# First mixer of a hybrid decoder step reordered: token mixing on GpSimd during the sort, second group of key scores behind the eighth head

## What is computed

```python
def ab_mixer(h, e, dsa_fn, shift_prev, S0, P):
    z = h @ P['ab_w_in'][e]
    q, k, v, qi, ki, wi, zb = split_cols(z, [...])
    ya = dsa_fn(e, q, k, v, qi, ki, wi)      # top-k keys by index scores, then softmax(q k) v over them
    yb, shift_new, S_new = rwkv7(zb, shift_prev, S0, e, P)
    y = jnp.concatenate([ya, yb], axis=-1) @ P['ab_w_out'][e]

def rwkv7(zb, shift_prev, S0, e, P):
    prev = jnp.concatenate([shift_prev[:, None], zb[:, :-1]], axis=1)
    z = zb + (prev - zb) * P['rwkv_mu'][e]                 # the token mixing
    r, k, v, xw, xa, xg = split_cols(z, [512] * 3 + [64, 64, 128])
    w_log = -softplus(-(w0 + tanh(xw) @ w2)) - 0.5         # decays
    a = sigmoid(a0 + xa @ a2)                              # rates
    g = sigmoid(xg) @ g2
    kk = k * P['rwkv_kk'][e]; kk = kk * rsqrt(max(sum(kk * kk), 1e-24))
    k = k * (1.0 + (a - 1.0) * P['rwkv_ka'][e])
    # scan over tokens with r, exp(-exp(w_log)), k, v, -kk, kk * a
```

## Time and profile before

| | |
|---|---|
| median of 3 runs | 1491.55 us (1486.3 to 1495.07) |
| the profiled execution | 1492.41 us |
| its span in the trace | 1490.6 us |
| PE busy | 95% of the span |
| DVE busy | 74% |
| ACT, POOL busy | 22%, 22% |
| granted TensorE clock, mean | 0.965 |

### The profile page before, as it was taken

The page is one execution under the profiler, slowest core; times in us unless marked ns, Lnnn a source line. Parts: engine busy times, 40 slices in busy tenths (PEclk is TensorE's granted clock), DMA queues, the critical chain, the costliest instruction groups (busy, mean ns, idle before and its releaser), DMA issues.

```text
span 1490.6 us, 28278 instructions
## 1 busy us (share of the span) xinstructions
PE 1420.3 (95%) x11458; PEld 1296.7 (87%) x11458; DVE 1096.9 (74%) x1410; ACT 327.1 (22%) x651; POOL 332.6 (22%) x277
## 2 busy tenths in 40 slices
PE   6999999999778998899999999999999999999997
PEld 6999999995333697899999999999997569999997
DVE  7977677667866746788777688768579577887764
ACT  3111102003323442221110221111202362211110
POOL 2533112001100011253321153322200002443210
PEclk9999999999977998999999999999999879999998
DMA  8443542665974102544427344426152315444142
GB/s 313 144 166 113 200 147 102 218 198 175 351 270 167 41 30 90 213 149 168 169 80 255 118 172 166 169 101 235 45 207 111 128 52 209 152 162 161 63 158 89
DMA packets 62699, 233.15 MB, mean 156 GB/s; under 512 B 9003, under 2 KB 18544, under 8 KB 45580
## 3 DMA queue, kind: packets, MB, share of 16 engines
q1 hardware_dynamic: 50426, 224.56, 41.9%
q10 hardware_dynamic: 11554, 6.37, 1.4%
q0 software_dynamic: 624, 0.87, 0.2%
HBM read 225.54 MB, written 6.10 MB: 155 GB/s over the span
## 4 chain that ended last, share of the span: by engine, by line
PE 49%; DVE 5%; POOL 2%; ACT 1%; DMA 1%; issue 1%; POOLq 0%; DVEq 0%; SPq 0%
PE psum L191 15%; PE psum L193 15%; PE psum L192 14%; DVE x L393 1%; DVE ring_r L186 1%; DVE pair_hi L177 1%; DMA ring<-in_w_gu 1%; DVE hidden_hi L389 1%; DVE rstd L297 1%; POOL hidden L305 0%; POOL hidden L307 0%; PE psum L351 0%; PE psum L2681 0%; DMA ring<-in_w_cd 0%; PE psum L235 0%
## 5 line engine op out<-in xcount | busy, mean ns | idle before, releaser
L191 PE MATMUL psum<-x_hi_r,pair_hi 128*128 128x288 f32 x1736 | 517.2, 298 | 5.5 <-DVE up L598 2.7
L193 PE MATMUL psum<-x_hi_r,ring_r 128*128 128x288 f32 x1736 | 515.8, 297 | 0.0
L192 PE MATMUL psum<-x_lo_r,pair_hi 128*128 128x288 f32 x1608 | 475.5, 296 | 0.0
L186 DVE TENSOR_TENSOR ring_r<-ring,pair_hi 128x2048 fp32r<-128x2048 f32 (+1 forms) x127 | 341.0, 2685 | 4.3
L191 PEld LDWEIGHTS psum<-x_hi_r,pair_hi 128*128 128x128 f32 x1736 | 329.6, 190 | 8.2 <-issue 7.7
L193 PEld LDWEIGHTS psum<-x_hi_r,ring_r 128*128 128x128 f32 x1736 | 329.2, 190 | 0.0
L192 PEld LDWEIGHTS psum<-x_lo_r,pair_hi 128*128 128x128 f32 x1608 | 304.0, 189 | 0.3
L191 PE MATMUL psum<-hidden_hi_r,down_hi 128*128 128x288 f32 x704 | 208.5, 296 | 0.0
L192 PE MATMUL psum<-hidden_r,down_hi 128*128 128x288 f32 x704 | 208.0, 295 | 0.0
L193 PE MATMUL psum<-hidden_hi_r,down_r 128*128 128x288 f32 x704 | 207.3, 294 | 0.0
L177 DVE CAST pair_hi<-ring 128x2048 fp32r<-128x2048 f32 (+1 forms) x126 | 161.2, 1279 | 11.0 <-DMA ring<-in_w_gu 9.8
(11 more groups left out here) (545 smaller groups left out, 1847.1 us busy)
## 6 DMA issues: line engine op xcount, KB each, us to landing
ring<-in_w_gu SPq DMA_DIRECT2D x88, 1024.0 KB, 4.8
down<-in_w_down SPq DMA_DIRECT2D x64, 704.0 KB, 4.3
ring<-in_w_ab SPq DMA_DIRECT2D x18, 1024.0 KB, 5.1
ring<-in_w_cd SPq DMA_DIRECT2D x12, 1024.0 KB, 6.0
ring<-in_cache_k SPq DMA_DIRECT2D x32, 256.0 KB, 4.6
index_keys<-in_cache_k SPq DMA_DIRECT2D x32, 256.0 KB, 7.8
index_keys<-in_cache_i ACTq DMA_DIRECT2D x64, 64.0 KB, 2.8
eight_pages_ds<-in_cache_v SPq DMA_DIRECT2D x16, 256.0 KB, 5.2
```

The source lines that it names most:

```text
L186: return eng.tensor_tensor(lo, a, hi.bitcast(F32), ALU.subtract)
L191: pe.matmul(out, w_hi, x_hi, start=start, stop=False)
L192: pe.matmul(out, w_hi, x_lo, start=False, stop=False)
L193: return pe.matmul(out, w_lo, x_hi, start=False, stop=stop)
```

## The change

Token mixing moves from DVE to POOL: 27 tensor operations in place on slabs 16 to 29, two slabs at a time, each waiting for the one before, behind POOL's loads and beside the sort. DVE keeps only the copy of the last tokens, and ACT's tanh, PE's decay products and DVE's `inputs` wait for all 27. On PE the third value projection goes behind the sample index scores, which now wait for two value copies; the second group of key scores goes from head 6 to head 7. On DVE six rounds of the sort run ahead of head 0 and the query copies behind these; `ROUNDS` changes; the first half of `select` (now `threshold`, to L2023) goes ahead of head 7; the sampled softmax takes both groups together. In branch B the decays' products come before the weights' transposes and the rates' products between them; the key norms' square root comes behind the three Exp; AR and BK are made in another order; sequences 4 to 7 are multiplied together, four at a time and not two, with key norms in the middle. SP sends key pages 2 and 3 first and page 1 and value 0 behind the third value projection, which also ends later for POOL's memset and loads.

```diff
+    def mixing(pool):
+        pool.wait_ge(S["mix_loaded"], 16 * 9)
+        pool.wait_ge(S["shift_ready"], 1)
+        zz = z[:, 16:30]
+        n = 0
+        def step(out_, in0, in1, op):
+            nonlocal n
+            if n:
+                pool.wait_ge(S["mixed"], n)
+            pool.tensor_tensor(out_, in0, in1, op).then_inc(S["mixed"], 1)
+            n += 1
+        def rates(j0, j1, w):
+            return mu[:, j0:j1].rearrange("p (j a) -> p j a", a=1).to_broadcast([P, j1 - j0, w])
+        d = shared[:, 0:2 * (TP - 1)].rearrange("p (j t) -> p j t", j=2)
+        for j in range(0, 14, 2):
+            pair = zz[:, j:j + 2]
+            step(d, pair[:, :, 0:TP - 1], pair[:, :, 1:TP], ALU.subtract)
+            step(d, d, rates(j, j + 2, TP - 1), ALU.mult)
+            step(pair[:, :, 1:TP], pair[:, :, 1:TP], d, ALU.add)
+        first = shared[:, 0:14].rearrange("p (j a) -> p j a", a=1)
+        step(first, zz[:, :, 0:1], rates(0, 14, 1), ALU.mult)
+        step(zz[:, :, 0:1], zz[:, :, 0:1], first, ALU.subtract)
+        ds = shared[:, 0:14 * NS].rearrange("p (j n) -> p j n", j=14)
+        d4 = shared[:, 0:14 * NS].rearrange("p (j b t) -> p j b t", j=14, t=TS)
+        zs = zz[:, :, TP:NT].rearrange("p a (b t) -> p a b t", t=TS)
+        step(d4[:, :, :, 1:TS], zs[:, :, :, 0:TS - 1], zs[:, :, :, 1:TS], ALU.subtract)
+        step(d4[:, :, :, 0], shiftT[:, :, :], zs[:, :, :, 0], ALU.subtract)
+        step(ds, ds, rates(0, 14, NS), ALU.mult)
+        step(zz[:, :, TP:NT], zz[:, :, TP:NT], ds, ALU.add)
+        assert n == MIXED
...
+        sp.wait_ge(A["ms_done"], 1)
+        sp.dma_start(g2, c.ins["g2"]).then_inc(S["par_loaded"], 16)
...
-    def inputs(dve, ln):
...
-        dve.tensor_tensor(D[:, :, 1:TP], zz[:, :, 0:TP - 1], zz[:, :, 1:TP], ALU.subtract).then_inc(S["shift_ready"], 1)
...
-        for j in [12, 13, 4, 5, 6, 7, 0, 1, 2, 3, 8, 9, 10, 11]:
-            ins = dve.scalar_tensor_tensor(zz[:, j], D[:, j], mu[:, j:j + 1], zz[:, j], ALU.mult, ALU.add).then_inc(S["mixed"], 1)
-        dve.wait_ge(S["mixed"], 14)
+        dve.tensor_copy(zlast[:, :, 1:1 + NB], zz[:, :, TP + TS - 1:NT:TS]).then_inc(S["shift_ready"], 1)
+    def inputs(dve, ln):
...
+        dve.wait_ge(S["mixed"], MIXED)
+        dve.wait_ge(c.stored, 48)
+        ln(dve.tensor_scalar(omka, ka, -1.0, 1.0, ALU.mult, ALU.add))
...
+        dve.tensor_tensor(e3, e2, e1, ALU.subtract).then_inc(S["kk_max"], 1)
+        dve.wait_ge(S["lora_out"], 2 * HP)
+        for h in range(HP):
+            last = dve.tensor_scalar(f3[:, h], av[:, h], ka[:, h:h + 1], omka[:, h:h + 1], ALU.mult, ALU.add)
+        ln(last)
+        ln(dve.tensor_tensor(k, k, f3[:, :, :], ALU.mult))
...
+        def scaled(slot_of, a):
+            for q in range(2):
+                for c0, c1, n in ((0, 4, L), (4, 5, NS)):
+                    cols = slice(c0 * L, c0 * L + (c1 - c0) * n)
+                    last = dve.tensor_tensor(BK[half(q), :, c0:c1, slot_of(q), 0:n],
+                                             a[half(q), :, cols].rearrange("p h (c l) -> p h c l", l=n),
+                                             e2[half(q), :, cols].rearrange("p h (c l) -> p h c l", l=n), ALU.mult)
+            return last
+        dve.wait_ge(S["w_done"], 3)
+        dve.wait_ge(S["zeroed"], 2)
+        dve.tensor_tensor(AR[:, 1, :, 0:NT], r, e1, ALU.mult)
+        scaled(lambda q: 1 - q, k)
...
+        dve.scalar_tensor_tensor(AR[:, 0, :, 0:NT], f1[:, :, :], -1.0, e3, ALU.mult, ALU.mult).then_inc(S["ar_done"], 1)
+        ln(dve.tensor_tensor(f2[:, :, :], f1[:, :, :], av[:, :, :], ALU.mult))
+        scaled(lambda q: q, f2).then_inc(S["bk_done"], 1)
...
+    def decay_inputs(act):
+        act.wait_ge(S["mixed"], MIXED)
+        act.activation(decay_in, decay_in, ACT.Tanh).then_inc(S["lora_in"], 1)
     def lora_out(act):
...
+            act.wait_ge(S["lora_sum"], HP + h + 1)
+            act.activation(av[:, h], early[h][:, 0:NT], ACT.Sigmoid, bias=a0[:, h:h + 1]).then_inc(S["lora_out"], 1)
...
+        act.wait_ge(S["kk_max"], 2)
+        act.activation(rows8, rows8, ACT.Sqrt).then_inc(S["root_done"], 1)
...
     def decay_products(pe):
         pe.wait_ge(S["mix_loaded"], 16 * 9)
-        pe.wait_ge(A["st_out"], 6)
-        pe.wait_ge(S["lora_in"], 2)
+        pe.wait_ge(S["lora_in"], 1)
+        pe.wait_ge(A["mb_done"], 6)
...
-ROUNDS = (0, 3, 14, 17, 28, 31, 33, 33, 33)
+ROUNDS = (6, 10, 14, 23, 27, 31, 33, 33, 33)
...
+            for u in range(4):
+                sp.wait_ge(S["is_sum"], 3 * u + 2)
+                load("cache_k", 2 + u // 2, KEY_SLOTS[2 + u // 2], range(4 * (u % 2), 4 * (u % 2) + 4))
+            sp.wait_ge(S["is_used"], 12)
             sp.wait_ge(c.pair_done, first + npairs + 2)
             load("cache_k", 1, KEY_SLOTS[1])
+            load("cache_v", 0, VALUE_SLOTS[0])
+            idx.read_numbers(sp, c, 6)
+            idx.read_numbers(sp, c, 7)
             sp.wait_ge(v_done, 3)
             c.store(sp, c.outs["v_p"], vtok[:, 0:2])
...
             rk.lora_loads(pool)
+            rk.mixing(pool)
             rk.zeros(pool)
...
-            values_in(2, range(KT))
...
-            pe.wait_ge(v_done, 3)
+            pe.wait_ge(v_done, 2)
...
             weigh(11)
-            pe.wait_ge(S["wi_done"], 1)
+            values_in(2, range(KT))
...
-                if h in (2, 6):
+                if h in (2, 7):
                     key_scores(h // 4)
...
+            rk.decay_products(pe)
             pe.wait_ge(S["pt_out"], 8)
...
             weights_transposed(0)
             pe.wait_ge(S["st_out"], 3)
+            pe.wait_ge(v_done, 3)
             pages_landed(range(4))
             sample_values(range(4), range(4)).then_inc(S["kv_used"], 1)
+            rk.rate_products(pe)
             weights_transposed(1)
             sample_values(range(4), range(4, NPG + 1)).then_inc(S["kv_used"], 2)
-            rk.decay_products(pe)
+            rk.key_squares(pe)
             pe.wait_ge(S["st_out"], 6)
+            rk.rates_taken(pe)
             pages_landed((4, 5))
-            sample_values((4, 5), range(3))
-            rk.key_squares(pe)
-            sample_values((4, 5), range(3, 6))
-            rk.rate_products(pe)
-            sample_values((4, 5), range(6, NPG + 1)).then_inc(S["kv_used"], 1)
-            pages_landed((6, 7))
-            sample_values((6, 7), range(2))
+            pe.wait_ge(kv_landed[4], 256)
+            sample_values(range(4, 8), range(4))
             rk.key_norms(pe)
-            sample_values((6, 7), range(2, NPG + 1)).then_inc(S["kv_used"], 1)
+            pe.wait_ge(kv_landed[5], 256)
+            sample_values(range(4, 8), range(4, NPG + 1)).then_inc(S["kv_used"], 2)
             rk.value_products(pe)
             heads_transposed(0)
...
             keys_out(1)
+            rk.decay_inputs(act)
...
             weights_out(0)
+            rk.lora_out(act)
             weights_out(1)
-            rk.lora_inputs(act)
-            rk.lora_out(act)
             rk.decays(act)
...
+            def sample_queries():
+                dve.wait_ge(S["qz_zero"], 2)
+                rk.last_tokens(dve)
...
+            def select():
...
+            for i in range(ROUNDS[0]):
+                top_eight(i)
+            sample_queries()
             for h in range(8):
+                if h == 7:
+                    threshold()
                 head(h)
...
             masked(0)
+            masked(1)
             largest(0)
-            masked(1)
+            largest(1)
             divided(0)
-            largest(1)
             divided(1)
```

More of the change, by code:

```diff
@@ L755 @@
 EXP_HALF = float(np.exp(-0.5))
+MIXED = 27
 Recurrence = namedtuple("Recurrence", (
-    "first_loads", "lora_loads", "zeros", "restricted_keys", "sample_decays", "rows_load", "last_loads", "stores", "inputs", "chunks", "lora_inputs", "lora_out", "decays", "chunks_out",
+    "first_loads", "lora_loads", "zeros", "restricted_keys", "sample_decays", "mixing", "last_tokens", "rates_taken", "rows_load", "last_loads", "stores", "inputs", "chunks", "decay_inputs", "lora_out", "decays", "chunks_out",
     "decay_products", "key_squares", "rate_products", "key_norms", "value_products", "chunk_products"))
@@ L1161, in decay_products @@
         pe.wait_ge(S["mix_loaded"], 16 * 9)
-        pe.wait_ge(A["st_out"], 6)
-        pe.wait_ge(S["lora_in"], 2)
+        pe.wait_ge(S["lora_in"], 1)
+        pe.wait_ge(A["mb_done"], 6)
+        pe.wait_ge(A["op_out"], 4)
         for h in range(HP):
-            pe.matmul(free[h][:, 0:NT], wa2[0:64, h * P:h * P + P], lw[0:64, 0], start=True, stop=True).then_inc(S["lora_sum"], 1)
+            pe.matmul(early[h][:, 0:NT], wa2[0:64, h * P:h * P + P], decay_in, start=True, stop=True).then_inc(S["lora_sum"], 1)
     def key_squares(pe):
@@ L1177, in rate_products @@
             pe.wait_ge(S["lora_out"], h + 1)
-            pe.matmul(free[h][:, 0:NT], wa2[64:128, h * P:h * P + P], z[64:128, Z_WA], start=True, stop=True).then_inc(S["lora_sum"], 1)
```

(11 more changed lines are left out.)

86 lines of the change are left out of this document (26 added, 60 removed).

## The result

| | before | changed |
|---|---|---|
| median of 20 runs | 1495.25 us (1486.3 to 1499.01) | 1488.01 us (1478.72 to 1493.12) |
| ratio of the times | | 0.995, 95% interval 0.9933 to 0.9967 |
| profiled execution, its span | 1492.41, 1490.6 us | 1493.08, 1491.3 us |
| first index scores | 364.75 | 359.63 |
| sort begins / merge | 378.82 / 421.40 to 427.05 | 373.90 / 417.47 to 426.44 |

The change gains 7.2 us in the medians, 5 to 10 by the interval, half a per cent. The forecast was 1482 us, a gain of 9.55 on the median at hand. Of the 6 us between 1482 and 1488, 3.7 are the start: the median of the kernel before is 1495.25 over 20 runs and was 1491.55 over the three at hand. The other 2.3 are gain that did not come. 1488 also lies outside the 1479 to 1485 that the forecast case gave as its own, though well inside the whole range of 1473 to 1494.

A forecast was written before the change was run, and what follows sets the result against it. PE, busy 95%, bounds the kernel outside the mixers; inside, the chunk products' start decides. 1.6 us at the first sampled values plus 8.2 behind them give 9.8: profiled 1492.4 becomes 1482.6, forecast 1482 us, range 1473 to 1494.

The forecast's parts named there:

- the forecast case: The main case for the whole kernel: 1482 us, own range 1479 to 1485, chance 0.42.
- Index scores and sort: Mixer's start: index scores at 359.2, 5.5 us earlier; sort about 5.4 earlier; merge starts at 416.
- Mixing on GpSimd: Token mixing on POOL: starts at 395, takes 30 us (bounds 27.6 and 32), ends at 425.
- The disturbance: GpSimd's mixing beside VectorE's merge: each waits for the other's instruction; merge 12 us (5.6 to 14.6), sort untouched.
- The rival of a sort that waits for GpSimd: Sort and mixing run by turns, merge ends 15 us later; 1497 or 1510 us, middle 1502, chance 0.12.
- a merge without a collision: Rival: merge ends at 421.6, first sampled values 6.4 us earlier, 16 in all; 1475.5 us, chance 0.15.
- Key scores, pages, S: From the merge to the first sampled values (S): pages requested at 439.5, S at 459, against 460.58 before.
- M: The merge's end, forecast at 428, between 421.6 and 431; before it was 427.
- From S to the chunks: From first sampled values to chunk products: 36.5 us (34 to 39), before 44.7; 8.2 gained.
- a tail over 39: Sign of being wrong: more than 39 us from the first sampled values to the chunk products.
- PE's short idle in front of the key norms: Term between first sampled values and chunk products: 1.3 us added for TensorE's idle time.
- my second rival: Gain mostly given back: late mixing, full merge, half-clock key scores, S at 464 to 466; 1487 us, chance 0.27.

The follow-up runs named there:

- x2: Changed kernel with the token mixing on VectorE again, tanh, decay and rates' products behind the first group's sampled values; ratio to the kernel before 0.9948.
- x11: Changed kernel with five more unused GpSimd steps in front of the mixing; one execution, merge 13.0 us, chunk products at 501.3, no ratio given.
- x3: Changed kernel with the second group of key scores behind head 6 again; ratio to the kernel before 0.9964.
- x1: Changed kernel with VectorE's reciprocal of the key norms moved ahead of the first half of BK; ratio to the kernel before 0.9907.
- x6: Changed kernel with sequences 4 to 7 multiplied two at a time again; ratio to the kernel before 0.9934.
- x10: Changed kernel with reciprocal ahead of half of BK, mixing ahead of wa2's load, and sequences 4 to 7 two at a time; ratio to the kernel before 0.9945.
- x4: Changed kernel with GpSimd's mixing issued ahead of the load of wa2; ratio to the kernel before 0.9923.

## Why the prediction was right, and where it was not

**Right: the place, the sign and the range; in part by luck.** The chunk products' start was named as the sum's end. The mixer's last store is issued 5.9 us earlier than before (595.27 against 601.21), and of the 6.3 us at the chunks 5.5 are left when the next half of the layer takes its first gate (643.49 against 648.99); the medians say 7.2.

**Index scores and sort: nearly.** The forecast had them at 359.2 (359.63), the sort from 373.4 (373.90) and the merge at 416 (417.47). The last is 1.5 late. The sum had 415.4 and 0.6 for the biases that meet POOL; they cost 1.4. The other 0.7 are not POOL's: with the mixing on VectorE (x2) the merge starts at 416.08, 0.7 behind the sum.

**Mixing on GpSimd: right.** 395 to 425 forecast, 394.81 to 423.98 measured. It is 29.2 long and lies nearer to the lower of the two bounds (27.6 and 32), since a subtraction of 510 elements took 1.03 us and an addition in place 1.19, not the 1.41 that the 288-element row gave:

```profile
394.81 1.03 POOL L868 TENSOR_TENSOR shared_ds<-z 128x510 f32<-128x510 f32 x1 [5.66 <-DMA cmask<-in_wa]
...
397.03 1.19 POOL L868 TENSOR_TENSOR z<-z,shared_ds 128x510 f32<-128x510 f32 x1
...
422.73 1.25 POOL L868 TENSOR_TENSOR z<-z,shared_ds 128x448 f32<-128x448 f32 x1
```

**The disturbance: right mechanism, price too high.** I took 12 us for the merge and it was 9.0. The experiments give 0.5 to 0.7 us for each us of overlap. At 9.0 the merge stayed below the 10 to 14 that the prediction had named as its sign. My upper bound had every GpSimd step delay the merge in full, and 9 us of overlap where there were 6.5. The sort was untouched, as I took it. Its groups from 394 to 417 us, beside the mixing (count, busy us, mean ns, idle before):

```profile
L2025 DVE MAX8 z<-z 128x8 f32<-128x264 f32 x18 | 7.8, 434 | 0.4
L2028 DVE MATCH_REPLACE8 z<-z 128x264 f32<-128x264 f32 x17 | 7.1, 417 | 0.0
```

In x2, where POOL is idle in that stretch, the means are the same 434 and 417 ns. The rival of a sort that waits for GpSimd falls with these rows; that of a merge without a collision falls with x2 and x11.

**Key scores, pages, S: right in each term from M on.** M + 6.3 was M + 6.1, the request at M + 11.5 came at M + 11.3, and 19.5 from the request to S were 19.7. S is 1.6 earlier than forecast only because M is. In the changed kernel and all its edits but x3 the first values are released by a page, in the changed kernel 0.8 us behind the weights (457.39 against 456.58); in the kernel before it was the weights. "Reordering the sort gives hardly 2 us" measured 3.2 and hid two parts: 8.7 from the order, 5.5 given back by GpSimd's place.

**From S to the chunks: this step failed.** The forecast was 36.5, at most 39, and it measured 41.6; a tail over 39 was one of the prediction's own signs of being wrong. The term that was mis-sized is the 1.3 us "for PE's short idle in front of the key norms". The reciprocal came 1.3 later than in the sum (0.65 of it from ScalarE's last Exp, and L943 on VectorE, 0.45, stood in no term), PE was idle 3.3 us, and the clock fell to 0.50. The norms took 4.2 and not 2.2, and the products of sequences 4 to 7 with their last step 7.4 and not 4.4. 1.3 + 2.0 + 3.0 less the 1.3 allowed is 5.0, the whole miss. x1 shows it: with the idle time cut to 0.4 us the tail is 35.6. x6 shows that idle time and not the norms' own work brings the half clock: with the idle time filled the clock is 1.00. I had written down, from the earlier trace rows, that PE's idle time elsewhere is followed by half clock, and did not apply it to the one idle time that the change makes itself. "The four-fold products keep PE from taking its place" was wrong in the changed kernel (x6) and right once the idle time is gone (x10).

**The sum.** 9.8 forecast, plus 1.6 at S, less 5.1 in the tail, is the 6.3 measured. The two errors are of opposite sign, and the forecast of the time is better than that of its largest term: that is luck. A gain of 7.2 is also just under the 7.5 that the prediction called measurable, and so on the line between its "faster" and its "same"; with 20 runs of each the interval, 5 to 10 us, leaves no doubt of the sign. The measured 1488 is the time of my second rival (1487), but not its mechanism: that had the pages asked for late and S at 464 to 466, with the tail as forecast, and it was S that came early and the tail that was long.

## What to carry to other kernels

Where an engine that is about to starve sits in front of a meeting, count its idle time twice: once as it stands, and once as the half clock of what follows. A small instruction on another engine that lengthens it (2.85 us here) can cost twice its length, and added work that fills it can be free (x6), but not once the idle time is gone (x10). Work moved to GpSimd is free only while VectorE does work that does not contend with it; look at what VectorE does at the end of the moved work, not only at its start (here the merge, and not the sort), and start it as early as its data allow: 4 us earlier gave 2 (x4). Where executions differ by 14 us for reasons downstream, judge a local change by a local instant.

## What the runs showed of the hardware

GpSimd's steps did not lengthen MAX8, MATCH_REPLACE8 or reciprocals, but they did lengthen a bias of two elements per partition, with one input from SBUF, from 0.17 to 0.88 us, and copies between partitions of 256 columns from 0.28 to 1.26. The Trainium skill (page "SBUF — State Buffer", Who interferes with whom) excepts one-input instructions from contention only outside a two-port mode; the trace agrees for the sort. It names copies and `tensor_scalar` as operations that can enter such a mode; here the copies and the bias waited. Of the two instructions of 128 columns in each stage of the merge the first, behind a wait, paid (0.84 on average in x11) and the second did not (0.28); of those of 256 columns the second paid too (1.10 and 1.32).

The granted clock fell to 0.50 at the end of an idle time of 3.3 us of TensorE and stayed there for 10 us (changed kernel, 480 to 490). Behind one of 0.4 us (x1) the norms still ran at full clock, in 2.17 us, and it fell for 3.5 us after them. With no idle time (x6) it stayed at 1.00. In the second layer it fell, in the first profile of the changed kernel, at 1159.5, with TensorE busy throughout from 1150 to 1168. In the executions profiled it stayed low there for longer in some than in others, 13 us of the span between two of the same kernel.
